# A mixer block: pooling moved to VectorE, first taps and layer norm moved to ScalarE, paired scans, another order of the output projection

## The chip, the cores and the metric

The kernel runs on one core of a Trainium2 chip. The metric is the device time of one execution in microseconds (us). The core's engines work side by side, each through its own list of instructions, and wait for one another through semaphores: TensorE (PE in the rows; its weight loads are PEld), VectorE (DVE), ScalarE (ACT), GpSimd (POOL) and SyncE (SP), which here only issues the loads of weights.

## The reference, cut to what matters

The whole network is a Mamba-2 layer, an attention layer, a mixer layer with an MLP, and a final norm, over 512 tokens of width 1024. Only the mixer is changed. It puts 16 meta tokens ahead of the 512 (528 positions), and computes:

```python
p = u @ w_in                      # 1792 = 14 blocks of 128 columns
p_pool, p_bval, p_bgate, p_cgate, p_cx = jnp.split(p, splits, axis=-1)
y_a = _pool_mixer(p_pool, ...)    # sliding means of 2, 4, 8, 16 positions, minus u; a matmul by groups; a scale
y_b = _conformer_conv(p_bval, p_bgate, ...)
#     v*sigmoid(gate); causal depthwise conv of 31 taps; layer norm; silu; matmul 256x256
y_c = _rglru_branch(p_cgate, p_cx, ...)
#     conv of 4 taps; two gates; linear scan over positions; times gelu(gate)
h = h + concatenate([y_a, y_b, y_c]) @ w_out
```

Only the outputs of the last 512 positions are kept; the meta tokens matter through the convolutions and the scan.

## The kernel before

All matrices are float32, held transposed (128 channels on the partitions, positions along the row). A product by a large weight is three matmuls: the weight and the data are each split into a high part and a rest, `w_hi`, `w_lo`, `a_hi`, `a_lo` (`b_hi`, `b_lo` for the second operand buffer). For every unit, that is a 1024x128 block of weights, SyncE loads `w_raw`, ScalarE makes `w_hi` (line 919), VectorE makes `w_lo` (line 1344, the helper `lo`), and TensorE runs 24 matmuls per 512 columns (line 508, `tile_of`). Two units are in flight: the high part of unit n+2 waits until TensorE is done with unit n.

The mixer's input projection has 14 tiles, n = 0 to 13, each of 528 columns in two halves of 264. In order they hold: the convolution's values and gates (0 to 3), the recurrence's inputs (4 to 7), the pooling's inputs (8, 9), the recurrence's gates for the gelu (10 to 13). The order on every engine is written by hand:

- VectorE goes through steps n = 0 to 13: it evacuates tile n from PSUM (line 1877), makes the rest of the weights n+2 (line 1344), and then does a share of the remaining work: `long_tap`, one tap of the 31-tap convolution on 128x512 (line 1784; how many a step gets stands in `TAPS`), `short_conv` (4 taps, lines 1796 and 1801), `one_minus_a2` (line 1809), `scan` (two multiplications and the scan, lines 1816, 1818, 1819), `means` (the end of the pooling, lines 1832 and 1834), `layer_norm_sums` (lines 1846, 1849) and `layer_norm` (lines 1856, 1858). First taps are a scalar multiply and add (lines 1781 and 1796); all later ones accumulate. Behind the steps come the lower halves of the output projection's operand, `b_lo` (lines 1825, 1912, 1916).
- ScalarE makes `w_hi` of unit n+2 in step n, then the gates' sigmoids (line 1212), exponentials (1222, 1223, 1226), roots (1233), gelus (1238), the silu behind the layer norm (1270), and `b_hi` (1244, 1277, 1281).
- GpSimd makes the sliding sums (lines 462 to 469) and multiplies the scan's result by the gelu (line 479).
- TensorE puts the recurrence's gate matmuls (line 814) behind tiles 6, 7, 9 and 10, turns the convolution's result for the layer norm behind tile 12 (line 839), turns it back behind tile 13 (line 846), then does the pooling's matmuls (line 852), the 256x256 product (line 859), and the eight tiles of the output projection `out2`. `b_hi` blocks 0, 1 are the pooling's, 2, 3 the convolution's, 4 to 7 the recurrence's.

A wait such as `pe.wait_ge(S["dw_ready"], 2)` holds all that stands behind it on that engine. `dw_ready` comes with the last long tap of each half, `ln_ready` with the normalised values, `cs_ready` with the silu, `acc_read` with the evacuation of a tile, `yl_ready` with each block of `b_lo`.

Of the kernel before, what the change touches and what calls it, by code (L numbers as in the profile page):

```python
# [2093 lines left out]
```

## Time and profile before

| | us |
|---|---|
| median of 3 runs | 1343.14 (1342.62 to 1344.46) |
| the profiled execution, its own time | 1345.11 |
| its span | 1343.2 |
| granted TensorE clock over the span, as a share of full speed | 0.976 |
| TensorE busy | 1253.6 (93% of the span) |
| VectorE busy | 868.4 (65%) |
| ScalarE busy | 598.7 (45%) |
| GpSimd busy | 70.8 (5%) |

Times in the rows count from the start of the span. The mixer's steps 4 to 13 and what follows them up to the output projection lie between 833 and 927 us. A duration in a row of VectorE or ScalarE overlaps the next instruction a little: what an instruction takes in a row of its like is the distance between starts.

### The profile page before, as it was taken

The page shows a single profiled execution, that of the slowest core. Times are in us where ns is not written, and L with a number is a line of the kernel's source. Part 1 is how long each engine was busy: PE and PEld are TensorE (multiplying, and loading weights), DVE is VectorE, ACT ScalarE, POOL GpSimd, SP SyncE. Part 2 cuts the span into 40 slices and gives each one's busy share as a digit, 9 for nine tenths or more (in the row PEclk, how much of TensorE's full clock was granted, in tenths as well). Part 3 has the DMA queues.
Part 4 walks back from the last instruction along what each step waited for, and adds up shares of the span by engine and source line. Part 5 has one row for each costly group of instructions (what it writes and reads, how often), then busy time and mean ns, then how long its engine had stood idle before and what let it go on. Part 6 is the DMA issues. An engine that isn't in the chain of part 4 may idle for free.

```text
span 1343.2 us, 17556 instructions
## 1 busy us (share of the span) xinstructions
PE 1253.6 (93%) x6213; PEld 1023.0 (76%) x6213; DVE 868.4 (65%) x1196; ACT 598.7 (45%) x909; POOL 70.8 (5%) x58
## 2 busy tenths in 40 slices
PE   7899999999988999999999699958999999999997
PEld 5687778777876887777777489956888888888885
DVE  4978888788873455666666667997655522455322
ACT  6456556655652344556556453444432211222112
POOL 0011110111011000000000000121000000000000
PEclk9999999999998999999999799979999999999999
DMA  5333233323323332222222032211333333333332
GB/s 154 109 97 110 79 94 96 107 78 94 98 74 86 94 94 79 69 74 66 74 62 63 26 97 82 64 47 48 94 94 94 94 94 94 94 94 94 110 94 78
DMA packets 203289, 115.57 MB, mean 86 GB/s; under 512 B 3456, under 2 KB 201216, under 8 KB 202224
## 3 DMA queue, kind: packets, MB, share of 16 engines
q1 hardware_dynamic: 201472, 104.50, 27.1%
q0 software_dynamic: 1776, 10.53, 2.3%
q8 instruction: 25, 0.41, 0.1%
q14 instruction: 16, 0.13, 0.0%
HBM read 112.85 MB, written 2.16 MB: 86 GB/s over the span
## 4 chain that ended last, share of the span: by engine, by line
PE 64%; DVE 23%; issue 6%; ACT 6%; DMA 1%; DVEq 0%; SPq 0%; ACTq 0%; POOL 0%
PE psum L508 59%; DVE w_lo L1344 4%; ACT w_hi L919 2%; DVE arena L1784 2%; DVE arena L1417 2%; DVE arena L1635 2%; DVE arena L1418 1%; DVE arena L1482 1%; PE psum L693 1%; DVE mixw L1506 1%; DVE mixw L1510 1%; DMA w_raw<-a_w_in 1%; ACT L1116 1%; ACT arena L1116 1%; DVE arena L1419 1%
## 5 line engine op out<-in xcount | busy, mean ns | idle before, releaser
L919 ACT ACTIVATE w_hi<-w_raw 128x1024 fp32r<-128x1024 f32 x191 | 202.2, 1059 | 520.8 <-PE psum L508 519.0
L508 PE MATMUL psum<-a_hi,w_hi 128*128 128x512 f32 (+1 forms) x1000 | 361.5, 380 | 5.8 <-DVE w_lo L1344 5.8
L508 PE MATMUL psum<-a_lo,w_hi 128*128 128x512 f32 (+1 forms) x1000 | 355.6, 374 | 0.0
L508 PE MATMUL psum<-a_hi,w_lo 128*128 128x512 f32 (+1 forms) x1000 | 353.8, 372 | 0.0
L1344 DVE TENSOR_TENSOR w_lo<-w_raw,w_hi 128x1024 fp32r<-128x1024 f32 x191 | 256.3, 1342 | 150.6 <-ACT w_hi L919 150.3
L508 PE MATMUL psum<-b_hi,w_hi 128*128 128x512 f32 x640 | 256.6, 401 | 8.0 <-DVE b_lo L1523 4.1
L508 PE MATMUL psum<-b_lo,w_hi 128*128 128x512 f32 x640 | 255.5, 399 | 0.0
L508 PE MATMUL psum<-b_hi,w_lo 128*128 128x512 f32 x640 | 254.0, 397 | 0.0
L508 PEld LDWEIGHTS psum<-a_hi,w_hi 128*128 128x128 f32 x1000 | 183.8, 191 | 43.5 <-issue 7.2
L508 PEld LDWEIGHTS psum<-a_hi,w_lo 128*128 128x128 f32 x1000 | 182.9, 191 | 33.9
L508 PEld LDWEIGHTS psum<-a_lo,w_hi 128*128 128x128 f32 x1000 | 182.9, 191 | 32.1
L508 PEld LDWEIGHTS psum<-b_hi,w_hi 128*128 128x128 f32 x640 | 121.7, 190 | 43.8 <-issue 5.6
L508 PEld LDWEIGHTS psum<-b_hi,w_lo 128*128 128x128 f32 x640 | 121.9, 190 | 28.0
L508 PEld LDWEIGHTS psum<-b_lo,w_hi 128*128 128x128 f32 x640 | 121.7, 190 | 27.3
L1948 DVE SCALAR_TENSOR_TENSOR arena<-psum,rt 128x512 f32<-128x512 f32 x32 | 22.1, 692 | 54.4 <-PE psum L508 52.5
L1963 DVE TENSOR_TENSOR h<-h,psum 128x512 f32 (+1 forms) x16 | 11.0, 688 | 59.2 <-PE psum L508 59.2
L1784 DVE SCALAR_TENSOR_TENSOR arena<-arena,par 128x512 f32<-128x512 f32 x60 | 45.2, 789 | 0.5
L1628 DVE TENSOR_TENSOR arena<-psum,rt 128x512 f32<-128x512 f32 x32 | 22.0, 688 | 30.6 <-PE psum L508 29.5
L1116 ACT ACTIVATE arena<-arena,stat 128x128 f32<-128x128 f32 (+3 forms) x64 | 35.4, 555 | 0.9
L951 ACT ACTIVATE arena<-arena,gconv 128x512 f32<-128x512 f32 x32 | 25.8, 805 | 20.9 <-DVE arena L1407 20.9
L1635 DVE SCALAR_TENSOR_TENSOR arena<-arena,stat,psum 128x128 f32<-128x128 f32 (+3 forms) x64 | 32.0, 541 | 4.3 <-PE psum L675 3.5
L1407 DVE TENSOR_TENSOR arena<-psum,rt 128x512 f32<-128x512 f32 x32 | 22.1, 690 | 18.8 <-PE psum L508 17.9
(264 smaller groups left out, 1259.7 us busy)
## 6 DMA issues: line engine op xcount, KB each, us to landing
w_raw<-a_w_in SPq DMA_DIRECT2D x49, 512.0 KB, 3.9
w_raw<-w_up SPq DMA_DIRECT2D x32, 512.0 KB, 3.9
w_raw<-w_down SPq DMA_DIRECT2D x32, 512.0 KB, 3.7
arena<-acs POOLq DMA_DIRECT2D x8, 1024.0 KB, 5.0
w_raw<-a_w_out SPq DMA_DIRECT2D x16, 512.0 KB, 3.7
w_raw<-w_kv SPq DMA_DIRECT2D x16, 512.0 KB, 3.9
w_raw<-b_w_in SPq DMA_DIRECT2D x16, 512.0 KB, 3.9
w_raw<-w_in SPq DMA_DIRECT2D x14, 512.0 KB, 3.8
```

Source lines behind the costliest of these rows:

```text
L508: ins = mm(out, wv[:, u.par, k, :], xv[:, k0 + k, c0:c0 + cn], start=(first and begin and i == 0 and n == 0), stop=(last and end and i == ...
L693: ins = mm(bank(7)[:, P * q:P * q + P], awt[:, q * (q + 1) // 2 + k, :], avt[:, s.par, k, :], start=(k == 0), stop=(k == q), skip_group_ch ...
L919: ac(w_hi[:, u.par, :, :], w_raw[:, u.par, :, :], ACT.Copy).then_inc(S["hi_ready"], 1)
L951: ac(conv[:, j % 2, :], pre[:, 3:3 + SEQ], ACT.Identity, scale=gconv[:, 5 * j + 3:5 * j + 4], bias=gconv[:, 5 * j + 4:5 * j + 5]).then_inc ...
L1116: ac(part, part, ACT.Exp, bias=stat_at(A_NB + 2 * q + i, 1), scale=0.125, accum_out=stat_at(A_SUM + 2 * q + i, 1)).then_inc(S["ex_ready"], 1)
L1344: tt(w_lo[:, u.par, :, :], w_raw[:, u.par, :, :], f32(w_hi[:, u.par, :, :]), ALU.subtract).then_inc(S["lo_ready"], 1)
L1407: tt(pre[:, 3:3 + SEQ], acc(m), rt[:, 0:SEQ], ALU.mult).then_inc(S["acc_read"], 1)
L1417: own.mark(stt(c, pre[:, 2:2 + SEQ], w[2], c, ALU.mult, ALU.add))
L1628: tt(dst, acc(n * 4 + (M_ATT + j)), rt[:, 0:SEQ], ALU.mult).then_inc(S["acc_read"], 1)
L1635: ins = stt(asc[:, at + n * i:at + n * i + n], dist[:, SEQ - n:SEQ], stat_at(SLOPE, 1), bank(2 + 2 * (q % 2) + i)[:, 0:n], ALU.mult, ALU.add)
L1784: ins = stt(dwo[:, j, :], src, w, dwo[:, j, :], ALU.mult, ALU.add)
L1948: stt(ft, acc(m + (M_MLP + 24 * half)), 0.0, rt[:, 0:SEQ], ALU.max, ALU.mult).then_inc(S["acc_read"], 1)
```

## The change

Six things change, all of them in the mixer.

1. **Pooling.** GpSimd's sliding sums and the halves of `means` go. `window_means` on VectorE does both blocks together in eight instructions of 512 to 526 columns, over all 128 partitions; the constant `upper` (1 on the upper 64 partitions) adds the wider window only there. The first 16 positions, whose outputs are dropped, are left out. It stands in step 11.
2. **Products.** The multiplication of the scan by the gelu goes from GpSimd to VectorE (`rnn_out`), behind the last step.
3. **First taps.** The first taps of the long and the short convolutions go to ScalarE (`first_tap_long`, `first_tap_short`), as an Identity with scale and bias.
4. **Layer norm.** The transposes of the convolution's result go from behind tile 12 to behind tile 11, into two PSUM banks that are free there, the sums to step 11, and the normalisation goes to ScalarE, as four activations of 256 columns with scale 1/sd and bias -mean/sd.
5. **Tiles 10 to 13** need only the last 512 columns: `in2_gate` runs 24 matmuls of 512 columns into one bank, in place of 48 of 264.
6. **Order.** `scans` takes two blocks of channels together, the 256x256 product comes before the pooling's matmuls, and the first two tiles of `out2` take blocks 4 to 7 first, then 0 to 3.

The core of the diff:

```diff
-                steps.mark(add(a[:, 1:n], u[:, 1:n], u[:, 0:n - 1], ALU.add))
-                steps.mark(add(b[:, 3:n], a[:, 3:n], a[:, 1:n - 2], ALU.add))
...
-            for j in range(4):
-                pool.wait_ge(S["ge_ready"], j + 1)
-                pool.wait_ge(S["scan_ready"], j + 1)
-                nc.gpsimd.tensor_tensor(xc[:, j, META:T2], xc[:, j, META:T2], cg[:, j, META:T2], ALU.mult).then_inc(S["yc_ready"], 1)
...
+            def in2_gate(n):
+
+                u, m = Lin(U_IN2 + n), Lin(M_IN2 + n)
+                pe.wait_ge(S["acc_read"], (m - 1).v)
+                pe.wait_ge(S["lo_ready"], (u + 1).v)
+                for k in range(KT):
+                    for i, (wv, xv) in enumerate(((w_hi, a_hi), (w_hi, a_lo), (w_lo, a_hi))):
+                        ins = mm(bank(2 * m.par), wv[:, u.par, k, :], xv[:, k, META:T2],
...
+            in2_gate(10)
+            gates(3)
+            in2_gate(11)
+
+            pe.wait_ge(S["dw_ready"], 2)
+            pe.wait_ge(S["acc_read"], M_IN2 + 10)
...
+            ins.then_inc(S["ln_tp"], 1)
+            in2_gate(12)
             pe.wait_ge(S["ln_ready"], 1)
+            pe.wait_ge(S["rga_ready"], 4)
...
             ins.then_inc(S["lnb_tp"], 1)
+            in2_gate(13)
...
-            out2(Lin(0), (4, 5, 6, 7, 0, 1), None, True, False)
-            out2(Lin(0), (2, 3), ("yl_ready", KT + 7), False, True)
-            out2(Lin(1))
+            out2(Lin(0), (4, 5, 6, 7), None, True, False)
+            out2(Lin(1), (4, 5, 6, 7), None, True, False)
+            out2(Lin(0), (0, 1, 2, 3), ("yl_ready", KT + 5), False, True)
+            out2(Lin(1), (0, 1, 2, 3), None, False, True)
...
                 if n == 11:
-                    gate_roots((2, 3))
-                if n == 12:
                     act.wait_ge(S["ln_stat"], 1)
                     root(stat_at(N_SD), bnag[:, :, 1], eps2, 1.0, S["ln_sd"])
+                    act.wait_ge(S["ln_shift"], 1)
+                    for i in range(NT):
+                        ins = ac(lnt[:, i, :], bank(1 + 2 * (i // 2))[:, 256 * (i % 2):256 * (i % 2) + 256],
+                                 ACT.Identity, scale=stat_at(N_RS + i, 1), bias=stat_at(N_R2 + i, 1))
+                    ins.then_inc(S["ln_ready"], 1)
+                    gate_roots((2, 3))
...
-            TAPS = {1: 3, 2: 5, 3: 4, 4: 1, 5: 1, 6: 1, 7: 1, 8: 8, 9: 10, 10: 10, 11: 6}
+            TAPS = {1: 2, 2: 5, 3: 3, 4: 1, 5: 1, 6: 1, 7: 1, 8: 8, 9: 10, 10: 16}
...
                 if n == 8:
-                    scan(0)
-                    scan(1)
-                if n == 10:
-                    means(0)
+                    scans(0)
                 if n == 11:
+                    window_means()
+                    layer_norm_sums()
                     one_minus_a2(2)
                     one_minus_a2(3)
+                    layer_norm_shift()
                 if n == 12:
-                    layer_norm_sums()
-                    scan(2)
-                    layer_norm()
-            means(1)
+                    scans(2)
             lo(Lin(U_OUT2 + 1))
-            scan(3)
+            for j in range(4):
+                rnn_out(j)
```

How the change moves instructions shows best on two engines. TensorE before, from tile 12 to the second tile of `out2`: line 508 is a tile of a projection, 839 the transposes ahead of the layer norm, 846 those behind it, 852 the pooling, 859 the 256x256 product.

```order
L508 MATMUL psum<-a_hi,w_hi 128x264 [waits lo_ready,acc_read]
...
L839 MATMUL psum<-con,arena 128x128 [waits dw_ready,rga_ready]
...
L508 MATMUL psum<-a_hi,w_hi 128x264 [waits lo_ready,acc_read]
...
L846 MATMUL psum<-con,arena 128x128 [waits ln_ready]
...
L852 MATMUL psum<-arena,mixw 128x512 [waits pool_ready,acc_read]
...
L859 MATMUL psum<-arena,mixw 128x512 [waits cs_ready]
...
L508 MATMUL psum<-b_hi,w_hi 128x512 [waits lo_ready,acc_read,yl_ready]
...
L508 MATMUL psum<-b_hi,w_hi 128x512 [waits yl_ready,lo_ready]
...
L508 MATMUL psum<-b_hi,w_hi 128x512 [waits lo_ready,acc_read]
```

TensorE after, from tile 11: line 781 is a tile of `in2_gate`, 825 and 834 the transposes ahead of the layer norm and behind it, 844 the 256x256 product, 851 the pooling, 479 `out2`.

```order
L781 MATMUL psum<-a_hi,w_hi 128x512 [waits lo_ready,acc_read]
...
L825 MATMUL psum<-con,arena 128x128 [waits acc_read,dw_ready]
...
L781 MATMUL psum<-a_hi,w_hi 128x512 [waits lo_ready,acc_read]
...
L834 MATMUL psum<-con,arena 128x128 [waits rga_ready,ln_ready]
...
L781 MATMUL psum<-a_hi,w_hi 128x512 [waits lo_ready,acc_read]
...
L844 MATMUL psum<-arena,mixw 128x512 [waits cs_ready]
...
L851 MATMUL psum<-arena,mixw 128x512 [waits pool_ready,acc_read]
...
L479 MATMUL psum<-b_hi,w_hi 128x512 [waits lo_ready,acc_read,yl_ready]
...
L479 MATMUL psum<-b_hi,w_hi 128x512 [waits lo_ready,acc_read]
...
L479 MATMUL psum<-b_hi,w_hi 128x512 [waits yl_ready,lo_ready]
```

The transposes ahead of the layer norm moved from between tiles 12 and 13 to between 11 and 12, those behind it from behind tile 13 to ahead of it, and the product that waits for `cs_ready` now stands ahead of the pooling's matmuls.

VectorE before, steps 11 to 13: line 1877 evacuates a tile, 1784 is a long tap, 1846 the sums of the layer norm, 1858 its normalisation.

```order
L1877 TENSOR_TENSOR arena<-psum,arena 128x528 [waits unit_done]
L1344 TENSOR_TENSOR w_lo<-w_raw,w_hi 128x1024 [waits hi_ready]
L1784 SCALAR_TENSOR_TENSOR arena<-arena,par 128x512 [waits dve_own] x6
L1809 SCALAR_TENSOR_TENSOR arena<-arena 128x528 [waits at_ready] x2
L1877 TENSOR_TENSOR arena<-psum,arena 128x528 [waits unit_done]
...
L1846 BN_STATS bnst<-psum 128x6 [waits ln_tp]
...
L1816 TENSOR_TENSOR arena<-arena 128x528 [waits rga_ready]
L1818 TENSOR_TENSOR arena<-arena 128x528 [waits mu_ready,dve_own]
L1819 SCALAR_TENSOR_TENSOR arena<-arena 128x528 [waits dve_own]
...
L1858 TENSOR_SCALAR arena<-psum,bnag,stat 128x256 [waits dve_own]
...
L1877 TENSOR_TENSOR arena<-psum,arena 128x528 [waits unit_done]
...
L1344 TENSOR_TENSOR w_lo<-w_raw,w_hi 128x1024 [waits hi_ready]
```

VectorE after, from the end of step 10 to step 13: line 1905 evacuates a tile, 1793 is a long tap, 1859 to 1871 is `window_means`, 1878 the sums, 1888 the shift of the layer norm, 1828 to 1837 are `scans`.

```order
L1793 SCALAR_TENSOR_TENSOR arena<-arena,par 128x512 [waits dve_own] x16
L1905 TENSOR_TENSOR arena<-psum,arena 128x512 [waits unit_done]
L1354 TENSOR_TENSOR w_lo<-w_raw,w_hi 128x1024 [waits hi_ready]
L1859 TENSOR_TENSOR arena<-arena 128x514
...
L1871 SCALAR_TENSOR_TENSOR arena<-arena,con 128x512 [waits dve_own]
L1878 BN_STATS bnst<-psum 128x6 [waits ln_tp]
...
L1819 SCALAR_TENSOR_TENSOR arena<-arena 128x528 [waits at_ready] x2
...
L1888 SCALAR_TENSOR_TENSOR stat<-bnag,stat 128x4 [waits dve_own]
L1905 TENSOR_TENSOR arena<-psum,arena 128x512 [waits unit_done]
...
L1828 TENSOR_TENSOR arena<-arena 128x528 [waits rga_ready] x2
...
L1837 SCALAR_TENSOR_TENSOR arena<-arena 128x528 [waits dve_own] x2
L1905 TENSOR_TENSOR arena<-psum,arena 128x512 [waits unit_done]
```

All long taps now end in step 10; between the last of them and the sums of the layer norm stand an evacuation, a `w_lo` and the eight instructions of `window_means`.

## Rows read from the trace of the kernel before

**Rows 1.** Busy time of the engines in two stretches: start:end, length, PE, PEld, DVE, ACT, POOL, granted clock, DMA.

```profile
877.00:904.80 27.80, 16.39 (x104) 15.39 (x104) 27.60 (x37) 9.88 (x12) 7.33 (x6) 0.75 0.19 57
904.80:927.40 22.60, 17.46 (x76) 12.74 (x76) 21.19 (x36) 14.20 (x21) 5.35 (x4) 0.81 0.16 47
```

**Rows 2.** TensorE in order of time: start, duration, what, idle before it and releaser.

```profile
877.14 3.86 PE L814 MATMUL psum<-arena,mixw 128*128 128x264 f32 x8 [3.56 <-ACT arena L1212]
...
904.85 1.94 PE L839 MATMUL psum<-con,arena 128*128 128x128 f32 x8 [11.31 <-DVE arena L1784]
...
915.47 1.09 PE L846 MATMUL psum<-con,arena 128*128 128x128 f32 x8 [1.34 <-DVE arena L1858]
...
918.88 2.44 PE L852 MATMUL psum<-arena,mixw 128*128 128x512 f32 x4 [2.32 <-DVE arena L1834]
...
921.12 4.85 PE L859 MATMUL psum<-arena,mixw 128*128 128x512 f32 x8
...
927.48 0.50 PE L508 MATMUL psum<-b_hi,w_hi 128*128 128x512 f32 x1 [1.51 <-DVE b_lo L1912]
```

**Rows 3.** Busy time in half microseconds; PEclk is the third number from the end.

```profile
875.50:876.00 0.50, 0.00 (x0) 0.00 (x0) 0.47 (x2) 0.49 (x2) 0.00 (x0) 0.84 0.00 0
...
882.50:883.00 0.50, 0.50 (x6) 0.50 (x5) 0.50 (x2) 0.50 (x1) 0.00 (x0) 0.83 0.00 0
...
923.50:924.00 0.50, 0.50 (x2) 0.19 (x1) 0.50 (x1) 0.00 (x0) 0.50 (x1) 0.87 0.00 0
```

**Rows 4.** Chain that ended last, two of its pieces: start, length, what.

```profile
846.60 5.85 PE psum L508 x48
...
927.48 22.74 PE psum L508 x97
```

**Rows 5.** VectorE in order of time: start, duration, what, count.

```profile
835.47 0.55 DVE L1796 TENSOR_SCALAR arena<-arena,par 128x528 f32<-128x528 f32 x1
...
863.26 3.11 DVE L1809 SCALAR_TENSOR_TENSOR arena<-arena 128x528 f32<-128x528 f32 x2
...
871.60 0.70 DVE L1816 TENSOR_TENSOR arena<-arena 128x528 f32<-128x528 f32 x1
...
873.07 1.26 DVE L1819 TENSOR_TENSOR_SCAN arena<-arena 128x528 f32<-128x528 f32 x1
...
874.25 0.68 DVE L1816 TENSOR_TENSOR arena<-arena 128x528 f32<-128x528 f32 x1
...
878.61 6.71 DVE L1784 SCALAR_TENSOR_TENSOR arena<-arena,par 128x512 f32<-128x512 f32 x10
...
885.24 0.70 DVE L1877 TENSOR_TENSOR arena<-psum,arena 128x528 f32<-128x528 f32 x1
...
895.35 0.71 DVE L1877 TENSOR_TENSOR arena<-psum,arena 128x528 f32<-128x528 f32 x1
...
897.58 7.12 DVE L1784 SCALAR_TENSOR_TENSOR arena<-arena,par 128x512 f32<-128x512 f32 x6
904.62 1.32 DVE L1809 SCALAR_TENSOR_TENSOR arena<-arena 128x528 f32<-128x528 f32 x2
...
908.74 1.42 DVE L1846 BATCH_NORM_STATS2 bnst<-psum 128x6 f32<-128x256 f32 x4
```

**Rows 6.** GpSimd in order of time, same columns, and the idle before.

```profile
862.19 2.10 POOL L462 TENSOR_TENSOR arena<-arena 128x543 f32<-128x543 f32 x1 [442.18 <-DVE arena L1877]
```

**Rows 7.** ScalarE in order of time, same columns.

```profile
861.04 1.05 ACT L919 ACTIVATE w_hi<-w_raw 128x1024 fp32r<-128x1024 f32 x1
...
916.07 1.15 ACT L1238 ACTIVATE arena<-arena 128x512 f32<-128x512 f32 x2 [0.78 <-DVE arena L1877]
917.23 1.28 ACT L1270 ACT_TABLE_LOAD   x1
918.53 1.45 ACT L1270 ACTIVATE arena<-psum,par 128x512 f32<-128x512 f32 x2
```

**Rows 8.** ScalarE, groups of one form: count, busy us, mean ns, idle before.

```profile
L1116 ACT ACTIVATE arena<-arena,stat 128x256 f32<-128x256 f32 x16 | 8.0, 501 | 0.3
```

More of the change, by code:

```diff
@@ new lines, in _ @@
+            pe.wait_ge(S["nrs_ready"], 2)
+            spread(bank(5), stat_at(N_RS), TOKENS1, S["nrb_ready"])
+            tp(bank(7)[:, 0:META], stat[0:META, N_R2 + 4:N_R2 + 5].to_broadcast([META, P]), ident[0:META, 0:META])
+            spread(bank(4), stat_at(N_R2), TOKENS1, S["nrb_ready"])
+            in2(1, ks=range(5, KT))
+            for n in range(2, 7):
+                in2(n)
+            pe.wait_ge(S["rr_ready"], 3)
+            gates(0)
+            in2(7)
+            gates(1)
+            in2(8)
@@ new lines, in _ @@
+            in2(9)
+            gates(2)
+            in2_gate(10)
[3 more added lines that the diff above has]
+            pe.wait_ge(S["acc_read"], M_IN2 + 10)
+            for i, (c0, cn) in enumerate(TOKENS1):
+                for j in range(2):
+                    ins = tp(bank(1 + 2 * (i // 2))[:, 256 * (i % 2) + P * j:256 * (i % 2) + P * j + P],
+                             dwo[:, j, c0:c0 + cn], ident)
+            ins.then_inc(S["ln_tp"], 1)
@@ L849, in _ @@
+            pe.wait_ge(S["cs_ready"], 2)
+            for j in range(2):
+                for k in range(2):
+                    ins = mm(bank(6 + j), pwt[:, k, j, :], dwo[:, k, 0:SEQ],
+                             start=(k == 0), stop=(k == 1), skip_group_check=True)
+            ins.then_inc(S["pwm_ready"], 1)
             pe.wait_ge(S["acc_read"], M_IN2 + 14)
@@ L854, in _ @@
             ins.then_inc(S["poolm_ready"], 1)
[L856 to L870 removed]
+            pe.wait_ge(S["yl_ready"], KT + 4)
+            out2(Lin(0), (4, 5, 6, 7), None, True, False)
+            out2(Lin(1), (4, 5, 6, 7), None, True, False)
+            out2(Lin(0), (0, 1, 2, 3), ("yl_ready", KT + 5), False, True)
+            out2(Lin(1), (0, 1, 2, 3), None, False, True)
             with pe.Fori(0, 3) as i:
@@ L1766, in _ @@
             dve.wait_ge(S["rr_ready"], 3)
-            taps = ([(0, k) for k in range(8)] + [(1, k) for k in range(4)]
+            taps = ([(0, k) for k in range(1, 8)] + [(1, k) for k in range(1, 4)]
                     + [(j, k + 8 - 4 * j) for k in range(23) for j in range(2)] + [(1, k) for k in range(27, DW_K)])
-            assert sorted(taps) == [(j, k) for j in range(2) for k in range(DW_K)], taps
+            assert sorted(taps) == [(j, k) for j in range(2) for k in range(1, DW_K)], taps
             last = [0, 0]
@@ L1791, in short_conv @@
             def short_conv(j):
-                dve.wait_ge(S["acc_read"], M_IN2 + 5 + j)
                 c = xc[:, j, :]
-                w = [par[:, C_RGW + 4 * j + k:C_RGW + 4 * j + k + 1] for k in range(4)]
-                own(ts(c, cxp[:, 3:3 + T2], w[3], par[:, C_RGB + j:C_RGB + j + 1], ALU.mult, ALU.add))
                 for k in (2, 1, 0):
@@ L1799, in short_conv @@
                     long_tap()
-                    own.upto(n)
-                    ins = stt(c, cxp[:, k:k + T2], w[k], c, ALU.mult, ALU.add)
+                    if k == 2:
+                        dve.wait_ge(S["xc0_ready"], j + 1)
+                    else:
+                        own.upto(n)
+                    at = C_RGW + 4 * j + k
+                    ins = stt(c, cxp[:, k:k + T2], par[:, at:at + 1], c, ALU.mult, ALU.add)
                     if k:
@@ L2026, in constants @@
             rows = slice(64 * half, 64 * half + 64)
-            con[rows, K_INV + 16 * t:K_INV + 16 * t + 16] = 1.0 / np.minimum(np.arange(1, 17), w)
             con[rows, K_WIN + t] = 1.0 / w
+    con[64:, K_UPPER] = 1.0
     con[:, K_SLOPE:K_SLOPE + HEADS] = -8.0 * 2.0 ** -np.arange(1.0, HEADS + 1)
```

182 lines of the change are left out of this document (81 added, 101 removed).

## The prediction

> **What bounds the kernel now.** I read the busy times by stretch first, then each engine in order of time from 833 to 928 us, and last the chain of waits. From the start of the output projection at 927.48 on, TensorE is busy without a gap worth naming [rows 2, 4]; the change reaches nothing there but the order inside the first two tiles. So the question is one number: when the output projection starts. Ahead of it the reader is to see VectorE busy 27.60 of 27.80 us and then 21.19 of 22.60, while TensorE is busy 16.39 and 17.46 [rows 1]: TensorE waits 3.56, 11.31, 1.34, 2.32 and 1.51 us [rows 2]. The longest wait, 11.31, is for the last long tap on VectorE. The waits cost twice, since the granted clock falls from 2.4 to 1.2 GHz: TensorE had stopped at 873.6 (877.14 less 3.56), the clock fell within 875.5 to 876.0, TensorE resumed at 877.14, and the clock came back within 882.5 to 883.0, 5.5 us after the resumption. In the last piece it was back at about 923.6, 4.7 us after the matmuls that began at 918.88 [rows 2, 3].
>
> **The change, up to the last long tap.** An instruction of VectorE that doesn't need its predecessor starts about 0.09 before that one's end: ten taps take 6.71, so 0.665 each; two-input operations of 0.70 take 0.61; w_lo takes 1.14; from the evacuation at 885.24 to that at 895.35 lie 0.61, 1.14, ten taps and `means`, so `means` is 1.7 [rows 5].
> - First taps: four of 0.46 leave steps 4 to 7 [rows 5], 1.8 us. But step 8 needs the w_hi that ScalarE starts at 861.04, behind its exponentials [rows 7], and line 1809 followed that w_lo at 863.26. ScalarE has one more activation ahead, so I take 863.6. The 1.8 us turn into a wait of VectorE: worth nothing. The two first taps of the long convolution lie in steps where TensorE's tiles set the pace: nothing too.
> - Step 8: line 1809 took 3.11 beside GpSimd's sum of 2.10 us that began at 862.19, and 1.32 without [rows 5, 6]: 1.8 gained. Eight taps 5.3. The two scans: one took 2.65, from 871.60 to 874.25, two 5.3; in pairs four multiplications at 0.61 and two scans at 1.18 (873.07 to 874.25), 4.8 [rows 5]. Evacuation 9 starts at 863.6 + 1.35 + 5.3 + 4.8 = 875.05.
> - Step 9 is 0.61 + 1.14 + 6.65 = 8.4: 883.45. Step 10 is 0.61 + 1.14 + 16 x 0.665, with 0.3 for the last taps, which need one another: 896.15. Before, the last tap ended at about 904.7 [rows 5]. **The taps are 8.5 us earlier**: 1.8 by step 8 and its scans, 1.7 as `means` leaves step 10, 2.8 because the six taps of 7.12 no longer run beside GpSimd (4.0 by the ten, and the 0.3; GpSimd is busy 7.33 in that stretch [rows 1, 5]), 0.45 for a w_lo beside it, 1.75 as evacuation 11 and its w_lo now stand behind.
>
> **From the last tap to the output projection.** Here things are put in series.
> - TensorE, idle since tile 11, starts the transposes at 896.3 at 1.2 GHz: 1.6 (1.94 with its end) [rows 2]. Tile 12 is now 24 matmuls of 512 columns: 97 took 22.74, so 5.6 against 5.85 for a wide tile at full clock [rows 4], 0.25 a tile, 1.0 for four. At half rate up to 901.6 it ends at about 905.
> - VectorE: evacuation 11 and w_lo, 897.9; `window_means`, no row has these shapes, but four are of the kind of 0.61 and four of the kind of 0.665, with some 0.25 where one needs the one before: 5.35, between 4.9 (all at 0.61) and 5.9 (each behind its predecessor's result, 0.735, as the two operations from 871.60 to 873.07), so 903.25. Nothing hides it: the sums of the layer norm stand behind. Sums 1.8 (1.42 for the first four) [rows 5], 905.05; line 1809 twice, 906.4, under which ScalarE's root lies; reciprocal and shift 0.45, 906.85.
> - ScalarE normalises with two pointer operands from PSUM. Nearest: 0.50 for 256 columns from SBUF [rows 8], 1.45 for two of 512 from PSUM [rows 7]. So 0.45 to 0.7 each; I take 0.48, 1.9 in all: 908.8.
> - TensorE had stopped at 905 and waits 3.8, longer than the 3.56 that was enough for the clock to fall. Transposes 1.6, 910.4; tile 13 at half rate to 914, then at full: 1.8 of 5.6 done, 917.8.
> - ScalarE, before the gelus, makes two roots (1.2) and w_hi (1.06): 911.05. VectorE waits for that w_hi 3.5 us behind evacuation 12 (907.5), then w_lo 1.14 and scans 4.8: 917.0. Evacuation 13 thus waits for the tile, 917.8 to 918.5.
> - ScalarE: w_hi and evacuation end at 918.8, gelus 1.15, table load 1.28, silu 1.45 [rows 7]: 922.7. Products and lower halves on VectorE (four at 0.61, then four behind ScalarE's copies) end near 925.7, under what follows.
> - TensorE has been idle for 4.9 us. The 256x256 product took 4.85, the first 2.5 of it at 1.2 GHz, so about 3.5 at full clock for four matmuls of 512 columns; the pooling's two are then 1.75 (2.24 from 918.88 to 921.12, some of it slow) [rows 2, 3]. Now both stand behind `cs_ready`, where before the pooling's stood ahead. The clock comes back 4.7 to 5.5 us after a resumption: 4.7 x 0.5 = 2.35 done, 1.15 at full, 5.8. So 928.5, and 1.75 more: **930.2**.
>
> Before, 927.48 [rows 2]. The two tiles of `out2` with blocks 4 to 7 first take 5.6 in place of waiting for the pooling's and the product's b_lo, which come some 3 us after 930.2: covered, as before they nearly were. **Sum: +2.7 us.** On the profiled execution's own 1345.11 (span 1343.2, 1.9 outside it) that is 1347.8; that execution lies 2.0 above the median, so I put the same difference on the median, 1343.14: **1345.8 us**.
>
> The clock, told by the rows: six runs of matmuls are cut apart by waits here, and I price three of them partly at 1.2 GHz. The Trainium skill, "TensorE: Matmul & The Clock Gate", section "HAM oscillation — how this bites in real kernels", says that short bursts of matmuls with waits between them let the clock fall again and again, so that each burst starts slow. By that rule the sum stands; without it the second rival below holds. The Trainium skill also speaks against moving the work to ScalarE: "ScalarE: Activation LUTs", section "Rules for kernel authors", wants multiply and add on VectorE. Its section on what a table load costs gives, as an estimate, 0.28 us + 0.833 ns a column and 0.09 more for the second pointer, less 0.09 of overlap: 0.49 for 256 columns. The sum would be +2.75 by it.
>
> **Rivals.**
> - *VectorE's gain reaches the end* (faster). For it: VectorE is 98% busy [rows 1], and 8.5 us are gone at the last tap. If no other engine made it wait, its list from 896.15 on, 1.75 + 5.35 + 1.8 + 1.35 + 0.45 + 1.75 + 4.8 + 1.75 + 2.4 + 2.4 = 23.8, would end at 919.95: 7.5 earlier, 1335.6. Against: tile 13, gelus, silu and the product each need the one before; silu would have to end by 914.7.
> - *The clock stays at 2.4 GHz* (no change). Tile 13 ends by 915.3, evacuation 13 follows the scans at 917.0, silu 921.5, product and pooling 5.25: 926.8, so -0.7, 1342.4. Against: waits of 3.8 and 4.9 us.
> - *ScalarE and the clock cost more* (slower for certain). Normalising at 0.7 an activation adds 0.9, and a product wholly at 1.2 GHz (7.0 in place of 5.8) 1.2: +4.8, 1347.9. It decides from the first tenths on, since the sum lies on the bound. A stall of VectorE on ScalarE's first taps would count only if over the 1.8 us of slack in step 8.
>
> **How the numbers follow.** A measurement of this kernel can tell about 0.2%, 2.7 us. The chain as computed: 0.62; the clock's instants alone move it, a return 1.3 us sooner or later in two places by 0.65 each, +1.4 to +4.0 (1344.5 to 1347.1), half of it beyond 0.2%. Clock stays: 0.12. Costs more: 0.15. Gain reaches the end: 0.11. So slower 0.31 + 0.15 = 0.46, within 0.2% 0.31 + 0.12 = 0.43, faster 0.11. The range goes from below the second rival, 1341.8, to 1348.2 above the third; it leaves out the faster case and a rest.
>
> **What the changed profile would show.** The transposes' wait for the last tap near 9.5 us, ending near 896; line 1809 at 1.3 for two in step 8; VectorE waiting some 1.8 us in step 8 and 3.5 before the w_lo of step 12; a wait of TensorE of 3.5 to 4 us for the normalised values and of 5 for the silu, with the clock at 1.2 GHz behind each; `out2` starting near 930. The prediction is wrong if TensorE reaches the product before 919, or if a wait for first taps shows on VectorE in steps 4 to 7 that is longer than 0.45 us each.

## The result and the profile after

| | before | after |
|---|---|---|
| median in the comparison, us | 1344.39 (20 runs) | 1347.07 (1343.41 to 1350.68, 20 runs) |
| ratio to before | | 1.0021, 95% interval 1.0012 to 1.0031 |
| span of the profiled execution, us | 1343.2 | 1347.2 |
| its own time, us | 1345.11 | 1348.84 |
| granted TensorE clock over the span | 0.976 | 0.972 |

The changed kernel is slower by 2.8 us (0.0021 of 1344.39), between 1.6 and 4.2. The two spans differ by 4.0. Where that arises is read from three places that both kernels have: a `w_hi` on ScalarE ahead of the mixer, a later one in the output projection, and the last transposes of the final norm. ScalarE in order of time in before, then in after (start, duration, what, idle before it and releaser):

```profile
789.54 1.06 ACT L919 ACTIVATE w_hi<-w_raw 128x1024 fp32r<-128x1024 f32 x1 [2.64 <-PE psum L508]
...
955.59 1.06 ACT L919 ACTIVATE w_hi<-w_raw 128x1024 fp32r<-128x1024 f32 x1 [3.37 <-PE psum L508]
```

```profile
790.27 1.06 ACT L908 ACTIVATE w_hi<-w_raw 128x1024 fp32r<-128x1024 f32 x1 [2.64 <-PE psum L479]
...
958.72 1.06 ACT L908 ACTIVATE w_hi<-w_raw 128x1024 fp32r<-128x1024 f32 x1 [3.36 <-PE psum L479]
```

From one to the other lie 166.05 us before and 168.45 after. I call this **the mixer's length**: it grew by 2.40. It is read from one execution of each kernel, so the median of many executions can differ from it, in the experiments below by some tenths up to 2 us. The first row is already 0.73 late, ahead of anything changed. So 0.73 is taken off below wherever a time of after is set beside one of before. The rest, 0.9, lies in the final norm, which the change doesn't touch. TensorE in before and in after:

```profile
1334.42 1.09 PE L904 MATMUL psum<-con,h 128*128 128x128 f32 x8 [2.24 <-DVE arena L1987]
1335.81 1.09 PE L904 MATMUL psum<-con,h 128*128 128x128 f32 x8 [0.29 <-DVE arena L1987]
```

```profile
1337.57 3.53 PE L893 MATMUL psum<-con,h 128*128 128x128 f32 x16 [2.25 <-DVE arena L2011]
```

Behind the same wait of 2.24 the sixteen transposes took 2.48 with their gap in the one execution and 3.53 in the other, 1.05 more, of which some 0.2 is made up again before the end. No instruction of the change stands there, and the length doesn't go with the kernel: it was 3.60 in e7, which is built on before, and 2.48 in e2, which is built on after.

Busy time of the engines in the two stretches of [rows 1], in after:

```profile
877.00:904.80 27.80, 18.26 (x63) 14.66 (x64) 27.59 (x42) 10.15 (x13) 0.00 (x0) 0.70 0.20 57
904.80:927.40 22.60, 13.59 (x40) 9.04 (x39) 15.84 (x28) 13.56 (x21) 0.00 (x0) 0.71 0.16 46
```

VectorE fell from 21.19 to 15.84 us in the second stretch, and GpSimd from 5.35 to nothing. TensorE fell too, from 17.46 to 13.59, and its clock from 0.81 to 0.71. VectorE's time was saved, and TensorE waits instead. TensorE in order of time, to be laid beside [rows 2]:

```profile
877.41 3.86 PE L796 MATMUL psum<-arena,mixw 128*128 128x264 f32 x8 [3.14 <-ACT arena L1201]
...
897.00 1.97 PE L825 MATMUL psum<-con,arena 128*128 128x128 f32 x8 [9.13 <-DVE arena L1793]
...
909.29 1.97 PE L834 MATMUL psum<-con,arena 128*128 128x128 f32 x8 [4.01 <-ACT arena L1272]
...
923.20 5.97 PE L844 MATMUL psum<-arena,mixw 128*128 128x512 f32 x8 [5.00 <-ACT arena L1280]
...
929.01 1.88 PE L851 MATMUL psum<-arena,mixw 128*128 128x512 f32 x4
930.32 0.80 PE L479 MATMUL psum<-b_hi,w_hi 128*128 128x512 f32 x1
```

The waits behind the last tap were 1.34, 2.32 and 1.51; now they are 4.01 and 5.00. The output projection starts 2.1 later than before (930.32 - 0.73 - 927.48), and its first matmul is longer than that of before by 0.3. VectorE in order of time, beside [rows 5]:

```profile
820.98 1.54 DVE L1793 SCALAR_TENSOR_TENSOR arena<-arena,par 128x512 f32<-128x512 f32 x2 [0.88 <-ACT arena L1240]
...
861.08 0.71 DVE L1903 TENSOR_TENSOR arena<-psum,arena 128x528 f32<-128x528 f32 x1 [0.59 <-PE psum L479]
863.20 1.23 DVE L1354 TENSOR_TENSOR w_lo<-w_raw,w_hi 128x1024 fp32r<-128x1024 f32 x1 [1.41 <-ACT w_hi L908]
864.34 1.32 DVE L1819 SCALAR_TENSOR_TENSOR arena<-arena 128x528 f32<-128x528 f32 x2
...
875.67 0.68 DVE L1903 TENSOR_TENSOR arena<-psum,arena 128x528 f32<-128x528 f32 x1
...
896.86 0.68 DVE L1905 TENSOR_TENSOR arena<-psum,arena 128x512 f32<-128x512 f32 x1
897.47 1.22 DVE L1354 TENSOR_TENSOR w_lo<-w_raw,w_hi 128x1024 fp32r<-128x1024 f32 x1
898.60 0.69 DVE L1859 TENSOR_TENSOR arena<-arena 128x514 f32<-128x514 f32 x1
...
903.95 1.42 DVE L1878 BATCH_NORM_STATS2 bnst<-psum 128x6 f32<-128x256 f32 x4
...
911.28 1.23 DVE L1354 TENSOR_TENSOR w_lo<-w_raw,w_hi 128x1024 fp32r<-128x1024 f32 x1 [3.40 <-ACT w_hi L908]
...
918.23 0.69 DVE L1905 TENSOR_TENSOR arena<-psum,arena 128x512 f32<-128x512 f32 x1 [0.94 <-PE psum L781]
```

ScalarE, beside [rows 7]:

```profile
854.63 0.83 ACT L1247 ACTIVATE arena<-arena,par 128x528 f32<-128x528 f32 x1
...
907.31 1.93 ACT L1272 ACTIVATE arena<-psum,stat 128x256 f32<-128x256 f32 x4 [1.20 <-DVE stat L1888]
...
919.25 1.13 ACT L1227 ACTIVATE arena<-arena 128x512 f32<-128x512 f32 x2
920.40 1.28 ACT L1280 ACT_TABLE_LOAD   x1
921.70 1.45 ACT L1280 ACTIVATE arena<-psum,par 128x512 f32<-128x512 f32 x2
```

And the granted clock in half microseconds, beside [rows 3] (third number from the end):

```profile
876.50:877.00 0.50, 0.00 (x0) 0.00 (x0) 0.50 (x1) 0.50 (x2) 0.00 (x0) 0.60 0.00 0
...
883.00:883.50 0.50, 0.50 (x2) 0.40 (x2) 0.50 (x2) 0.50 (x1) 0.00 (x0) 0.57 0.00 0
...
890.00:890.50 0.50, 0.00 (x0) 0.00 (x0) 0.50 (x2) 0.42 (x1) 0.00 (x0) 0.76 0.00 0
...
900.50:901.00 0.50, 0.50 (x4) 0.42 (x3) 0.50 (x2) 0.00 (x0) 0.00 (x0) 1.00 0.94 279
...
907.00:907.50 0.50, 0.00 (x0) 0.00 (x0) 0.47 (x3) 0.19 (x1) 0.00 (x0) 0.82 0.00 0
...
914.00:914.50 0.50, 0.50 (x3) 0.41 (x2) 0.50 (x2) 0.00 (x0) 0.00 (x0) 0.85 0.92 275
...
920.50:921.00 0.50, 0.00 (x0) 0.00 (x0) 0.50 (x2) 0.50 (x1) 0.00 (x0) 0.98 0.00 0
...
927.50:928.00 0.50, 0.50 (x2) 0.28 (x1) 0.00 (x0) 0.00 (x0) 0.00 (x0) 0.70 0.00 0
```

A value between 0.50 and 1.00 is a half microsecond in which the clock changed between its two levels, 1.2 and 2.4 GHz. Inside each of the two waits, of 4.01 and 5.00 us, it falls, and it comes back 4.9 us (914.15 - 909.29) and 4.6 us (927.8 - 923.2) after the matmuls resume.

### The profile page after: what moved, and what is told of

Same layout as the page of the kernel before. It is cut to its first block, busy times and chain, and to the rows that moved or that the text cites. A ratio compares the mean times of both kernels' runs of the same rounds, so it can differ in the third digit from the quotient of the medians.

```text
span 1347.2 us, 17353 instructions
## 1 busy us (share of the span) xinstructions
PE 1255.0 (93%) x6117; PEld 1020.5 (76%) x6117; DVE 860.4 (64%) x1191; ACT 604.8 (45%) x919; POOL 53.4 (4%) x44
## 4 chain that ended last, share of the span: by engine, by line
PE 64%; DVE 23%; ACT 6%; issue 6%; DMA 0%; DVEq 0%; ACTq 0%; POOL 0%; SPq 0%
PE psum L479 58%; DVE w_lo L1354 4%; ACT w_hi L908 2%; DVE arena L1793 2%; DVE arena L1427 2%; DVE arena L1645 2%; DVE arena L1428 1%; PE psum L664 1%; DVE arena L1492 1%; DVE mixw L1516 1%; DVE mixw L1520 1%; ACT L1105 1%; DVE arena L1429 1%; ACT arena L1105 1%; DVE stat L1649 1%
## 5 line engine op out<-in xcount | busy, mean ns | idle before, releaser
L479 PE MATMUL psum<-a_hi,w_hi 128*128 128x512 f32 (+1 forms) x936 | 346.2, 384 | 3.6 <-DVE w_lo L1354 3.6
L479 PE MATMUL psum<-a_lo,w_hi 128*128 128x512 f32 (+1 forms) x936 | 340.7, 378 | 0.0
L479 PE MATMUL psum<-a_hi,w_lo 128*128 128x512 f32 (+1 forms) x936 | 339.6, 377 | 0.0
L479 PEld LDWEIGHTS psum<-a_hi,w_hi 128*128 128x128 f32 x936 | 172.1, 189 | 40.7 <-issue 7.2
L479 PEld LDWEIGHTS psum<-a_hi,w_lo 128*128 128x128 f32 x936 | 171.7, 189 | 33.6
L479 PEld LDWEIGHTS psum<-a_lo,w_hi 128*128 128x128 f32 x936 | 171.8, 189 | 31.9
```

What stands on the lines that cost most here:

```text
L479: ins = mm(out, wv[:, u.par, k, :], xv[:, k0 + k, c0:c0 + cn], start=(first and begin and i == 0 and n == 0), stop=(last and end and i == ...
```

## The experiments

Each ran beside the kernel before. The ratio is of the times; the column behind it is what the profile of one execution gives for the mixer's length against 166.05. Below, "shorter" and "longer" go by that length unless a ratio is named.

| experiment | base | median, us | ratio, 95% interval | mixer's length |
|---|---|---|---|---|
| the change | | 1347.07 | 1.0021 (1.0012 to 1.0031) | +2.40 |
| e1 pooling's sums late | after | 1343.43 | 0.9996 (0.9984 to 1.0009) | -1.62 |
| e2 pooling's matmuls first | after | 1343.68 | 1.0005 (0.9993 to 1.0016) | +0.12 |
| e3 filled waits | after | 1342.89 | 0.9996 (0.9984 to 1.0008) | -1.33 |
| e4 silu early | after | 1341.95 | 0.9982 (0.9969 to 0.9995) | -2.80 |
| e5 = e1 + e4 | after | 1338.61 | 0.9962 (0.9951 to 0.9973) | -5.90 |
| e6 first taps on ScalarE | before | 1344.16 | 1.0001 (0.9992 to 1.0011) | -0.64 |
| e7 no sums on GpSimd | before | 1340.54 | 0.9972 (0.9960 to 0.9984) | -4.59 |
| e8 = e5 + step 8 reordered | after | 1335.74 | 0.9949 (0.9929 to 0.9968) | -7.18 |
| e9 first taps on VectorE | after | 1347.32 | 1.0029 (1.0015 to 1.0044) | +2.60 |
| e10 = e8 + filled wait | after | 1336.47 | 0.9951 (0.9937 to 0.9964) | -8.74 |

**e1, the pooling's sums behind the layer norm.** In step 11 of VectorE:

```diff
-                    window_means()
                     layer_norm_sums()
                     one_minus_a2(2)
                     one_minus_a2(3)
                     layer_norm_shift()
+                    window_means()
```

> The changed kernel with one edit: the eight instructions of window_means stand behind the layer norm's shift in step 11, not ahead of its sums. VectorE has the same work. Series theory (what VectorE gained at the last tap is lost because the layer norm, tile 13, gelus, silu and the product each wait for the one before): normalised values some 4 us earlier, TensorE's wait for them nearly gone, the output projection 4.4 us earlier than in the changed kernel, so 1.7 us faster than the kernel before (ratio 0.9987). Work theory (the sum of VectorE's work sets the end, and the pooling on VectorE costs what it takes): no change against the changed kernel, ratio 1.002.

The mixer is shorter than after's by 4.0 (4.4 expected). The wait of 4.01 ahead of the second transposes is gone, but the one for the silu grew. TensorE:

```profile
919.78 6.49 PE L844 MATMUL psum<-arena,mixw 128*128 128x512 f32 x8 [7.05 <-ACT arena L1280]
```

So the 5.35 us of `window_means` lay on the path, and were worth 4.0 of it. The ratio fell from the changed kernel's 1.0021 to 0.9996; that the kernel is also faster than before, as I had expected (0.9987), the times don't show.

**e2, the pooling's matmuls ahead of the product again**, with everything else as changed:

```diff
-            pe.wait_ge(S["cs_ready"], 2)
...
-            ins.then_inc(S["pwm_ready"], 1)
             pe.wait_ge(S["acc_read"], M_IN2 + 14)
             pe.wait_ge(S["pool_ready"], 2)
...
             ins.then_inc(S["poolm_ready"], 1)
+            pe.wait_ge(S["cs_ready"], 2)
...
+            ins.then_inc(S["pwm_ready"], 1)
```

> The changed kernel with one edit: TensorE does the pooling's matmuls ahead of the 256x256 product, as in the kernel before. Series theory: the pooling's 1.75 us lie under the wait for the silu, and the product begins with a shorter idle time behind it: 2.7 us earlier than the changed kernel, ratio to before 1.000. Work theory: the order does not matter, ratio 1.002. If only the 1.75 us are won and the clock is not touched, ratio 1.0007.

```profile
918.46 1.98 PE L844 MATMUL psum<-arena,mixw 128*128 128x512 f32 x4 [0.78 <-DVE arena L1905]
...
922.69 5.40 PE L851 MATMUL psum<-arena,mixw 128*128 128x512 f32 x8 [2.24 <-ACT arena L1280]
```

The mixer is 2.28 shorter than after's (2.7 expected): the pooling's 1.72 went into the wait, and the product behind it took 5.40 in place of 5.97. Undoing this one exchange takes back all but 0.12 of the slowdown. Its ratio, 1.0005 (0.9993 to 1.0016), agrees with that, but can't tell the rest of 0.12 from nothing.

**e3, the waits filled** by matmuls of 256 columns whose results nobody reads, 8 behind tile 12 and 10 behind tile 13:

```diff
+            pe.wait_ge(S["rga_ready"], 4)
+            for _ in range(8):
+                mm(bank(6)[:, 0:256], pwt[:, 0, 0, :], con[:, 0:256], start=True, stop=True, skip_group_check=True)
             pe.wait_ge(S["ln_ready"], 1)
...
             in2_gate(13)
+            for _ in range(10):
+                mm(bank(6)[:, 0:256], pwt[:, 0, 0, :], con[:, 0:256], start=True, stop=True, skip_group_check=True)
```

> The changed kernel with 18 more matmuls whose results nobody reads (constant operands, 256 columns, a free bank): 8 behind tile 12, where TensorE waits for the normalised values, and 10 behind tile 13, where it waits for the silu. They hold TensorE busy and move nothing else. Clock theory (the two waits cost mostly because the matmuls behind them run at 1.2 GHz): clock at 2.4 GHz through tile 13 and the product, 3.4 us less than the changed kernel, ratio to before 0.9994. If the clock is of no account: 0, or a little slower by the fill's own end; ratio 1.002 to 1.003.

```profile
903.50:924.50 21.00, 18.95 (x80) 13.99 (x79) 15.33 (x27) 13.69 (x21) 0.00 (x0) 1.00 0.18 51
...
907.68 1.09 PE L837 MATMUL psum<-con,arena 128*128 128x128 f32 x8 [0.46 <-ACT arena L1277]
...
920.27 3.70 PE L849 MATMUL psum<-arena,mixw 128*128 128x512 f32 x8 [1.59 <-ACT arena L1285]
```

The first line is TensorE's stretch from the fill to the output projection, at a granted clock of 1.00 throughout. The chain of data is as in after, and only the clock differs: the transposes take 1.09 in place of 1.97, the product 3.70 in place of 5.97. The mixer is 3.73 shorter (3.4 expected). That is what the low clock costs in these two places, more than the whole slowdown.

**e4, the silu ahead of the gelus.** ScalarE's silu moves from behind step 13 into step 12, so that it no longer waits for tile 13:

```diff
+                if n == 12:
+                    act.wait_ge(S["lnb_tp"], 1)
+                    for j in range(2):
+                        ac(dwo[:, j, 0:SEQ], bank(4 + j), ACT.Silu,
...
-            act.wait_ge(S["lnb_tp"], 1)
-            for j in range(2):
-                ac(dwo[:, j, 0:SEQ], bank(4 + j), ACT.Silu,
...
```

> The changed kernel with one edit: ScalarE does the silu in step 12, ahead of all four gelus, in place of behind them; the number of table loads stays. Series theory: cs_ready comes near 914 in place of 923, the product starts right behind tile 13 with no idle time and the clock up, and the output projection then waits for the recurrence's blocks: 5 us less than the changed kernel, ratio to before 0.9983. Rival, the work of ScalarE is only moved and the gelus, now 2.7 us later, make VectorE's products late by as much: ratio 1.001 to 1.002.

The mixer is 5.20 shorter than after's (5 expected), and the times say the same: 0.9982 against 1.0021. What TensorE waits for ahead of `out2` is now the recurrence's `b_lo` from VectorE:

```profile
924.93 0.50 PE L479 MATMUL psum<-b_hi,w_hi 128*128 128x512 f32 x1 [2.13 <-DVE b_lo L1850]
```

**e5, both moves together**, e1's in VectorE's step 11 and e4's in ScalarE's step 12:

```diff
+                    act.wait_ge(S["lnb_tp"], 1)
...
                     layer_norm_shift()
+                    window_means()
```

> The two edits of e1 and e4 together: window_means behind the layer norm's shift, and the silu ahead of the gelus. Series theory: no chain through the layer norm is left ahead of the output projection, TensorE reaches the product near 912 without a wait for the silu, and VectorE's list sets the end as in the kernel before, only shorter: out2 starts near 921.4 on the clock of the trace before (927.48 there), 6 us faster than before, ratio 0.9955. Rival, the gains of e1 and e4 are the same microseconds twice: no more than e4 alone, ratio 0.998.

```profile
919.98 0.55 PE L479 MATMUL psum<-b_hi,w_hi 128*128 128x512 f32 x1 [3.84 <-DVE b_lo L1850]
...
919.50:921.00 1.50, 1.02 (x3) 0.88 (x4) 1.50 (x3) 0.80 (x2) 0.00 (x0) 0.76 0.00 0
921.00:924.00 3.00, 3.00 (x9) 2.29 (x9) 2.10 (x4) 0.00 (x0) 0.00 (x0) 0.55 0.02 5
```

The mixer is 5.90 shorter than before, 8.30 shorter than after. The two moves were worth 4.0 and 5.2 alone. From step 8 on VectorE's list now sets the start of the output projection, as in the first rival. That start comes 7.45 earlier than before (this execution runs 0.05 ahead of before's where the mixer begins), and the rival had put it at 7.5. Only 5.90 of it reach the end, because the clock falls behind the wait of 3.84 and the first matmuls of `out2` run at 1.2 GHz, up to about 923.7 (the last two lines); e10 prices the same place at 1.56. So my 6 us hit by luck: I had the start 1.4 later than it came, and no slow clock behind it.

**e6, the first taps alone, in the kernel before:**

```diff
+            def first_tap_short(j):
+                act.wait_ge(S["acc_read"], M_IN2 + 5 + j)
+                at = C_RGW + 4 * j + 3
+                ac(xc[:, j, :], cxp[:, 3:3 + T2], ACT.Identity, scale=par[:, at:at + 1],
...
-                own(ts(c, cxp[:, 3:3 + T2], w[3], par[:, C_RGB + j:C_RGB + j + 1], ALU.mult, ALU.add))
```

> The kernel before with the first taps alone moved to ScalarE. My theory: the 1.8 us that four short taps take off VectorE in steps 4 to 7 turn into a wait of VectorE for the w_hi of step 8, which ScalarE starts behind its exponentials; the step after it begins no earlier, mixer within 0.3 us, ratio 1.000. Rival, VectorE's work sets the pace throughout: 1.8 to 2.8 us faster, ratio 0.998 to 0.9985.

A miss, of 0.3 beyond my interval: -0.64. Its step 8 on VectorE:

```profile
862.76 2.03 DVE L1361 TENSOR_TENSOR w_lo<-w_raw,w_hi 128x1024 fp32r<-128x1024 f32 x1 [1.46 <-ACT w_hi L919]
864.71 1.36 DVE L1826 SCALAR_TENSOR_TENSOR arena<-arena 128x528 f32<-128x528 f32 x2
```

The taps' time became a wait, as said. But GpSimd's sum, which had met line 1809 and made it 3.11, now meets the `w_lo`, which grows from 1.23 to 2.03 only, while line 1826 takes 1.36. The eight taps behind line 1826 start 0.65 earlier by this, counted from the mixer's start, and that is the whole gain; the times can't tell it from nothing.

**e7, the kernel before without GpSimd's sliding sums.** Four lines, which make six additions, are left out, so the pooling's values aren't computed:

```diff
-                steps.mark(add(a[:, 1:n], u[:, 1:n], u[:, 0:n - 1], ALU.add))
-                steps.mark(add(b[:, 3:n], a[:, 3:n], a[:, 1:n - 2], ALU.add))
-                if j == 1:
-                    steps.mark(add(a[:, 7:n], b[:, 7:n], b[:, 3:n - 4], ALU.add))
-                    steps.mark(add(b[:, 15:n], a[:, 15:n], a[:, 7:n - 8], ALU.add))
```

> The kernel before with GpSimd's sliding sums left out (six additions over 529 to 543 columns; the short multiplications behind them stay, so the pooling's values are not computed). Theory: VectorE's two-input instructions run slow only beside them, line 1809 in step 8 goes from 3.11 to 1.3, the six taps of step 11 from 7.12 to 4.1, the w_lo ahead of them from 1.69 to 1.22: out2 starts 5 us earlier, ratio 0.9963. Rival, those instructions are slow for another reason: ratio 1.000.

```profile
863.17 1.37 DVE L1804 SCALAR_TENSOR_TENSOR arena<-arena 128x528 f32<-128x528 f32 x2
...
895.27 4.56 DVE L1779 SCALAR_TENSOR_TENSOR arena<-arena,par 128x512 f32<-128x512 f32 x6
```

Line 1809's pair falls from 3.11 to 1.37 and the six taps from 7.12 to 4.56 [rows 5]: 1.7 and 2.6, against 1.8 and 2.8 in the prediction. The six taps had been expected at 4.1 here. The mixer is 4.59 shorter (5 expected), the kernel 3.8 us faster (0.9960 to 0.9984). Taking the sums from GpSimd thus was worth 4 to 5 us; the change spent them again on the 5.35 us of `window_means`.

**e8, step 8 reordered, on top of e5**: two of its eight taps stand ahead of the `w_lo`, in VectorE's wait for `w_hi`.

```diff
-            TAPS = {1: 2, 2: 5, 3: 3, 4: 1, 5: 1, 6: 1, 7: 1, 8: 8, 9: 10, 10: 16}
+            TAPS = {1: 2, 2: 5, 3: 3, 4: 1, 5: 1, 6: 1, 7: 1, 8: 6, 9: 10, 10: 16}
...
+                if n == 8:
+                    long_tap()
+                    long_tap()
                 if 0 < n < 13:
                     lo(Lin(U_IN2 + n + 2))
```

> e5 with one more edit: in step 8 VectorE does two of the step's eight long taps ahead of the w_lo that waits for ScalarE, not behind it. If the 1.8 us of the first taps are lost in that wait, as I hold, about 1.3 of them come back: last tap 1.3 us earlier than in e5, ratio to before 0.9945, e5 less 1.3 us. Rival: the w_lo becomes late for TensorE's tile 10, or the scans still start by ScalarE's roots: no gain over e5.

```profile
857.22 1.41 DVE L1794 SCALAR_TENSOR_TENSOR arena<-arena,par 128x512 f32<-128x512 f32 x2
858.72 1.23 DVE L1355 TENSOR_TENSOR w_lo<-w_raw,w_hi 128x1024 fp32r<-128x1024 f32 x1
```

The wait of 1.45 is gone, and the mixer is 1.28 shorter than e5's (1.3 expected). With VectorE as the bound, closing a gap of 1.45 in its list far upstream brings 1.28. The times lie the same way, 0.9949 against 0.9962, but their intervals overlap, with 6 executions of e8.

**e9, the first taps back on VectorE**, in the changed kernel (the reverse of e6):

```diff
-                    first_tap_long(n // 2)
-                if 4 <= n < 8:
-                    first_tap_short(n - 4)
...
+                own(ts(c, cxp[:, 3:3 + T2], par[:, C_RGW + 4 * j + 3:C_RGW + 4 * j + 4],
...
```

> The changed kernel, with all first taps back on VectorE, everything else as changed. My theory: the four short first taps (0.46 each, 1.84) only fill VectorE's waits in step 8 (0.59 before the evacuation, 1.41 for the high part), and ScalarE's high part comes sooner without them: the weight's rest of step 8 starts 0.3 earlier to 0.2 later than in the changed kernel, counted from the mixer's start, and the mixer's length changes by -0.3, within -0.6 to +0.3; the two waits of 0.88 in steps 1 and 3 are gone. Rival: VectorE's list sets the pace here, and the 1.84 less the 0.59 come back: +1.25 or more.

```profile
860.72 1.23 DVE L1337 TENSOR_TENSOR w_lo<-w_raw,w_hi 128x1024 fp32r<-128x1024 f32 x1 [0.16 <-ACT w_hi L908]
```

The four taps' 1.84 us took the place of 1.84 us of waits: 0.59 ahead of the evacuation, and 1.41 less 0.16 ahead of the `w_lo`. The mixer is 0.20 longer than after's, inside what I had expected (-0.6 to +0.3). The waits of 0.88 are gone, without effect. So the first taps are worth nothing here, on either engine.

**e10, e8 with six matmuls of 256 columns behind the pooling's**, in TensorE's last wait:

```diff
             ins.then_inc(S["poolm_ready"], 1)
+            for _ in range(6):
+                mm(bank(5)[:, 0:256], pwt[:, 0, 0, :], con[:, 0:256], start=True, stop=True, skip_group_check=True)
```

> The version with the sums' late pooling, the early silu and step 8 reordered, and six products of 256 columns into a free bank (not part of the computation) behind the pooling's matmuls, in the last wait of 3.3 us. My theory: the output projection starts when it did, since VectorE's list sets that, but the clock doesn't fall inside it, where it stood at 1.2 GHz for 3.1 us: -1.5 us against that version, 0.9938 of the kernel before. Rival 1: the wait is VectorE's alone and the clock costs nothing any more: 0. Rival 2: the products take longer than the wait and push the output projection back: up to +1.

Clock of e8, and of e10, where the output projection starts:

```profile
914.00:917.00 3.00, 2.00 (x8) 1.65 (x9) 3.00 (x6) 1.32 (x3) 0.00 (x0) 0.92 0.00 0
917.00:920.00 3.00, 3.00 (x9) 2.32 (x8) 1.12 (x2) 0.00 (x0) 0.00 (x0) 0.51 0.02 5
```

```profile
921.00:924.00 3.00, 2.96 (x13) 2.43 (x14) 3.00 (x5) 0.37 (x1) 0.00 (x0) 1.00 0.00 0
```

In e8 the clock falls about 1.5 us after `out2` has started (915.00) and is low up to 919.95. In the profile the output projection starts at the same distance from the mixer's start as in e8, and the mixer is 1.56 shorter, as expected. The times don't show it: 0.9951 (0.9938 expected) against 0.9949, with intervals that reach 0.0014 and 0.0020 to either side. Whether it counts over many executions stays open.

## Why the prediction was right

The forecast was +2.7 us with 46 in 100 for slower; the times gave +2.8, the mixer's length +2.40. Two things in this are luck. The forecast lay on the prediction's own line between slower and unchanged (0.2%), and 0.21% is hardly over it. And by its own reckoning the clock's instants alone could have moved the sum between +1.4 and +4.0. The chain itself is not luck: e1 to e4 each take out one link of it, and each takes back 2.3 to 5.2 us. Its steps, each with 0.73 taken off the time of after:

- **Up to the last tap.** Evacuation 9 at 874.94 (predicted 875.05), evacuation 11, which follows the last tap, at 896.13 (896.15). The 1.8 of step 8 and the 2.8 of the taps for GpSimd were 1.7 and 2.6 in e7. The first taps were worth nothing, e9. VectorE waited 0.59 and 1.41 in step 8 (predicted some 1.8). Two waits of 0.88 in steps 1 and 3, behind the long convolution's first taps on ScalarE, I had not named; e9 removed them, at no gain.
- **`window_means` in front of the sums.** 898.60 to 903.95, 5.35 as predicted. It costs the end 4.0 (e1). The eight instructions had no row in before; the two distances taken from rows of their kind, 0.61 and 0.665, held, and 0.25 for the dependences too.
- **The normalisation on ScalarE.** 1.93, 0.48 for one (predicted 1.9 and 0.48). TensorE's wait 4.01 (3.8), VectorE's for `w_hi` 3.40 (3.5). TensorE had ended tile 12 at 904.55 (about 905; the prediction's own terms add up to 905.35).
- **Tile 13.** Its first matmuls were issued behind the transposes, which began at 908.56 (908.8), and it ended at 917.5 (917.8). The silu ended at 922.4 (922.7); TensorE had waited 5.00 (4.9).
- **Product and pooling.** 5.97 and 1.72, counted from end to end (5.8 and 1.75). e2 showed that the exchange of the two is worth 2.28.
- **The clock.** It fell in both waits and came back 4.9 and 4.6 us after the resumption, where I had used 4.7 to 5.5. e3 priced it: 3.73 us. The second rival, a clock that stays at 2.4 GHz, had put the kernel at -0.7; e3 measured -1.33 with it, so that rival was 0.6 too high, and its condition didn't hold in the changed kernel. The Trainium skill has the rule that short bursts of matmuls with waits between them start slow each time ("TensorE: Matmul & The Clock Gate", section "HAM oscillation — how this bites in real kernels"). The trace of after agrees: behind each of its waits of 3.14, 9.13, 4.01 and 5.00 us the matmuls started at 1.2 GHz; in before those behind the wait of 1.34 started at 2.4. One place went the other way: behind the first transposes at 897.00 the clock was back by 900.5, after 3.5 us and not 5.3. Tile 12 thus ended 0.4 before the "about 905" of the prediction, which its successors, waiting for VectorE, couldn't use.
- **The faster rival.** VectorE's gain of 8.5 us did not reach the end as the change stands. e5 shows what held it: the places of two groups of instructions. With `window_means` behind the shift and the silu ahead of the gelus, the output projection starts 7.45 earlier than before and the mixer is 5.90 shorter, with step 8's gap closed 7.18. So the moves as a whole were good, and their order took the gain back. The rival's "98% busy" is a misreading of [rows 1]: 27.60 and 21.19 of 50.40 us are 97%, and only 94% in the second stretch, where the chain lies.
- **The signs of being wrong.** "If TensorE reaches the product before 919" can only mean that it starts the product, which it did at 922.47; it stood in front of it from 917.5 on, as the prediction's own 917.8 has it.

The first taps were tried alone (e6, e9), the places of the sums, the product and the silu as well (e1, e2, e4); the layer norm's and the products' moves and the 512-column tiles never were, so what each of these is worth by itself isn't shown. In the rows two scans in a pair took 4.79 from start to start (870.88 to 875.67) where two single ones had taken 5.28, the 0.5 that the prediction had put in. What the difference between +2.40 and the predicted 2.7 is made of isn't shown either; it is within the tenths by which the terms above are off.

## What to carry to other kernels

When the busiest engine is relieved, list what each later wait is for and put the work that this chain needs first: here 5.35 us of sliding sums stood ahead of the layer norm's sums, for which ScalarE and TensorE waited, and a silu whose input was ready stood behind gelus whose input wasn't. Where the clock falls in a wait of TensorE, add the slow stretch behind it to the price (here 3.73 us behind two waits of 4.01 and 5.00), and place independent matmuls inside the wait and not behind it. A gap on an engine costs nothing until that engine sets the end (e6, e9); look at it again when it does (e8).

## What the runs showed of the hardware

- A granted clock that fell came back at different distances from the resumption in the trace of after: 3.5 us (897.00 to 900.5), 4.6, 4.9 and 6.0 (877.41 to 883.4). It fell 2.0 us after the matmuls had stopped at 905.3, and 2.3, 2.4 and 2.8 after the other three stops (874.3, 887.9 and 918.2).
- It can also fall when the wait is already over. In before it fell at 920.24, 1.4 us after the pooling's matmuls had begun behind a wait of only 2.32 (the line below); in e2 1.2 us after the product had begun behind a wait of 2.24; in e5 and e8 0.3 and 1.5 us after `out2` had begun behind waits of 3.84 and 3.30. In e6, with the same wait of 2.32 as in before, it fell inside the wait, and the pooling's matmuls took 3.75 in place of 2.44. So equal waits in two executions cost unequal time, and one trace doesn't tell what a wait of this length costs.

```profile
920.00:920.50 0.50, 0.50 (x2) 0.24 (x2) 0.50 (x1) 0.50 (x2) 0.00 (x0) 0.72 0.00 0
```

- GpSimd's addition with two operands, beside a two-operand instruction of VectorE, made six taps take 7.12 in place of 4.56 and a pair of line 1809 3.11 in place of 1.37, but a `w_lo` of 1024 columns only 2.03 in place of 1.23. The Trainium skill ("GPSIMD Engine Reference", section "Specifications") says that GpSimd shares its SBUF interfaces with VectorE and that instructions with two SBUF inputs contend. e7 agrees, and gives the size in this kernel: 3.8 us by the times, 4.59 by the mixer's length.
- A multiply and add by two pointers took ScalarE 0.83 us on 528 columns, against 0.55 on VectorE [rows 5]: slower by half, and free where ScalarE waits.
